# VectorE waits twice for POOL's low parts in the down product, and evicts the first turn ahead of the sums of h

## The reference

```python
def swiglu(h, w_gate, w_up, w_down):
    return (jax.nn.silu(h @ w_gate) * (h @ w_up)) @ w_down
...
    for l in range(DEPTH):
        x = x + 0.5 * swiglu(rms_norm(x, norm_ffn1[l]), ffn1_w_gate[l], ffn1_w_up[l], ffn1_w_down[l])
        ...  # recurrent branch, chunked attention, merge
        x = x + 0.5 * swiglu(rms_norm(x, norm_ffn2[l]), ffn2_w_gate[l], ffn2_w_up[l], ffn2_w_down[l])
```

## Time and profile before

| what | value |
|---|---|
| time, median of 3 runs | 2613.52 us (2612.52 to 2614.4) |
| the profiled execution, its time | 2616.7 us |
| its span, first to last instruction | 2614.9 us |
| granted TensorE clock, mean | 0.994 of full speed |
| PE busy | 2583.0 us, 99% of the span |
| DVE, ACT, POOL busy | 1402.8, 1145.6, 1147.1 us |

### The profile page before, as it was taken

The page is one execution under the profiler, slowest core; times in us unless marked ns, Lnnn a source line. Parts: engine busy times, 40 slices in busy tenths (PEclk is TensorE's granted clock), DMA queues, the critical chain, the costliest instruction groups (busy, mean ns, idle before and its releaser), DMA issues.

```text
span 2614.9 us, 32912 instructions
## 1 busy us (share of the span) xinstructions
PE 2583.0 (99%) x13244; PEld 2168.7 (83%) x13244; DVE 1402.8 (54%) x1949; ACT 1145.6 (44%) x1691; POOL 1147.1 (44%) x458
## 2 busy tenths in 40 slices
PE   9999999999999999999999999999999999999999
PEld 7999787878876788997888988877888778898977
DVE  8767326751346357764187681458413453677720
ACT  5334336743546443334243342467435463433431
POOL 4435544455431344536444354444454314434463
PEclk9999999999999999999999999999999999999999
DMA  5322734433323232422334323253233232424222
GB/s 164 122 73 85 229 91 117 107 96 105 99 73 94 86 113 89 126 69 89 98 91 128 94 69 107 81 134 102 84 110 94 70 100 89 121 68 126 73 93 77
DMA packets 258669, 263.77 MB, mean 101 GB/s; under 512 B 9574, under 2 KB 243174, under 8 KB 258518
## 3 DMA queue, kind: packets, MB, share of 16 engines
q1 hardware_dynamic: 253178, 251.65, 32.1%
q10 hardware_dynamic: 5340, 10.02, 1.3%
HBM read 252.25 MB, written 10.57 MB: 101 GB/s over the span
## 4 chain that ended last, share of the span: by engine, by line
PE 85%; DVE 9%; ACT 2%; POOL 2%; DMA 1%; issue 1%; SPq 0%; ACTq 0%; DVEq 0%
PE ps L1650 21%; PE ps L1654 21%; PE ps L1655 21%; PE ps L1758 4%; PE ps L1763 4%; PE ps L1762 4%; POOL wlo L579 2%; PE ps L1930 1%; PE ps L1988 1%; PE ps L2003 1%; DVE scan L1454 1%; DVE gates L1226 1%; PE ps L1948 1%; PE ps L1952 1%; PE ps L1953 1%; DVE scan L1446 1%
## 5 line engine op out<-in xcount | busy, mean ns | idle before, releaser
L579 POOL TENSOR_TENSOR wlo<-raw,whi 128x1024 fp32r<-128x1024 f32 x386 | 998.0, 2596 | 1029.1 <-ACT whi L623 1029.1
L1650 PE MATMUL ps<-h_lo,whi 128*128 128x512 f32 x1632 | 639.7, 392 | 8.2 <-DVE y L1386 5.6
L1654 PE MATMUL ps<-h_hi,whi 128*128 128x512 f32 x1632 | 637.2, 390 | 0.0
L1655 PE MATMUL ps<-h_hi,wlo 128*128 128x512 f32 x1632 | 637.2, 390 | 0.0
L623 ACT ACTIVATE whi<-raw 128x1024 fp32r<-128x1024 f32 x386 | 403.8, 1053 | 515.7 <-PE ps L1650 456.9
L1650 PEld LDWEIGHTS ps<-h_lo,whi 128*128 128x128 f32 x1632 | 307.5, 188 | 78.1 <-issue 14.2
L1655 PEld LDWEIGHTS ps<-h_hi,wlo 128*128 128x128 f32 x1632 | 307.5, 188 | 64.8
L1654 PEld LDWEIGHTS ps<-h_hi,whi 128*128 128x128 f32 x1632 | 307.6, 189 | 62.6
L1650 PE MATMUL ps<-act_lo,whi 128*128 128x512 f32 x704 | 278.4, 396 | 13.9 <-POOL wlo L579 13.9
L1654 PE MATMUL ps<-act_hi,whi 128*128 128x512 f32 x704 | 277.4, 394 | 0.0
L1655 PE MATMUL ps<-act_hi,wlo 128*128 128x512 f32 x704 | 276.8, 393 | 0.0
(11 more groups left out here) (232 smaller groups left out, 4374.1 us busy)
## 6 DMA issues: line engine op xcount, KB each, us to landing
raw<-in_w_in SPq DMA_DIRECT2D x124, 512.0 KB
raw<-in_w_up SPq DMA_DIRECT2D x88, 512.0 KB
raw<-in_w_down SPq DMA_DIRECT2D x80, 512.0 KB
w_a<-in_w_gate SPq DMA_DIRECT2D x60, 512.0 KB, 5.3
tmp<-in_w_gate SPq DMA_DIRECT2D x20, 512.0 KB, 7.2
rel_band<-rel_rows ACTq DMA_DIRECT2D x1, 8192.0 KB, 39.2
raw<-in_w_up_b SPq DMA_DIRECT2D x16, 512.0 KB
raw<-in_w_out SPq DMA_DIRECT2D x16, 512.0 KB
```

The costliest lines, as they stand in the source:

```text
L579: nc.gpsimd.tensor_tensor(wlo[:, s, :], src, whi[:, s, :].bitcast(F32), ALU.subtract).then_inc(lo_made, 1)
L1650: ins = pe.matmul(ps[:, b, :], w_hi, x_lo, start=start, stop=False)
L1654: pe.matmul(ps[:, b, :], w_hi, x_hi, start=False, stop=False)
L1655: return pe.matmul(ps[:, b, :], w_lo, x_hi, start=False, stop=stop)
```

## The change

ACT's list: the high part of the fifth down chunk moves up, to behind the high parts of tiles 12 to 15; one chunk fewer is then rounded in the loop over the pairs. VectorE's list: after the low parts of tiles 4 to 11 it waits until POOL has counted the low part of the fourth down chunk (`down_low(l, f, AHEAD)` is that count of `lo_made`), then makes the low parts of tiles 12 to 15, then multiplies the four tiles of the last unit as before, then waits for the low part of the fifth down chunk and makes the low parts of tiles 16 to 21. All this in each of the four blocks. `tees` is cut in two: `gains_made` (the eight tiles hx) and `tees` (the sums T and the low part of T2). In the first block alone the second half, and the low part of T1, come after `up_scaled` of the first turn.

```diff
                 act_high(4)
                 ring()
-                act_high(KF - 12)
+                act_high(4)
+                ring()
+                act_high(KF - 16)
                 if behind:
                     behind()
                 for j in range(KD // 2):
-                    ring(len(G22) - (1 if j == 0 else 0) - (AHEAD if ends and j == KD // 2 - 1 else 0))
+                    ring(len(G22) - (2 if j == 0 else 0) - (AHEAD if ends and j == KD // 2 - 1 else 0))
...
+            def down_low(l, f, n):
+
+                first = 4 + UNITS * (UPS + 3)
+                block = first + (KD // 2) * len(G22)
+                return SLOTS + l * (2 * block + MIX_CHUNKS) + f * (block + MIX_CHUNKS) + first + n + 1
...
-            def tees(gain):
+            def gains_made(gain):
 
                 for t in range(KD):
                     nc.vector.tensor_scalar(hx[:, t, :], x[:, t, :], gain(t), None, ALU.mult
                                             ).then_inc(t_step, C.made(t_step))
                 dve.wait_ge(t_step, C.now(t_step))
+
+            def tees():
+
...
-                t_low(T1, 3)
+                if (l, f) != (0, 0):
+                    t_low(T1, 3)
                 for m in range(2):
                     up_scaled(m, 2 + m)
+                if (l, f) == (0, 0):
+                    tees()
+                    t_low(T1, 3)
                 for m in range(2):
                     up_gated(m, m, C.next(silu_made))
...
                     if last:
                         act_low(4, 12)
+                        dve.wait_ge(lo_made, down_low(l, f, AHEAD))
+                        act_low(12, 16)
                     for m in range(4):
                         up_gated(t + m, m, C.next(silu_made, 4) - 1 if m == 0 else C.now(silu_made))
...
-                act_low(12, KF)
+                dve.wait_ge(lo_made, down_low(l, f, AHEAD + 1))
+                act_low(16, KF)
...
-                tees(lambda t: next_gain[:, t:t + 1])
+                gains_made(lambda t: next_gain[:, t:t + 1])
+                if l:
+                    tees()
...
-                tees(lambda t: col("ffn2", t))
+                gains_made(lambda t: col("ffn2", t))
+                tees()
```

## The result

The changed kernel takes 2592.79 us (median of 4 runs, 2590.13 to 2593.64), the kernel before 2613.96 beside it: a ratio of 0.9918, 95% interval 0.9901 to 0.9935, or 21.2 us. Forecast were 2590.3 us and faster. The profiled execution of the changed kernel took 2593.64, its span 2591.8.

A forecast was written before the change was run, and what follows sets the result against it. TensorE, busy 99% of the span, bounds the kernel; its largest wait is for POOL's low parts. 2616.7 - 23.8 + 0.6 = 2593.5 us profiled, 3.2 above the median, so 2590.3 against 2613.52; range 2585 to 2600.

The forecast's parts named there:

- POOL is shut out while VectorE's stream lasts, and a pause lets it in: Fourth down chunk, each block: POOL's subtraction, released by VectorE's wait, ends at 259.90 instead of 268.33 in the first block.
- POOL's longest subtraction near 2.9: Sign that the forecast holds: POOL's longest subtraction takes near 2.9 us and not 11.7.
- The port rule: Skill page: VectorE with two SBUF inputs and GpSimd share a port pair; whoever starts first fully blocks the other for that instruction.
- the margin of 0.2 us: Down product, first block: ACT's fifth high part ready at 259.70, just before POOL ends the fourth low part at 259.90.
- The second rival: Down product: VectorE gets memory first after the fourth low part, later POOL alternates with tiles 16 to 18; 2614 to 2621; chance 0.06.
- VectorE stays ahead: Down product, tiles 16 to 21: VectorE makes one per 0.60 us, TensorE takes one per 0.68, so TensorE sees no cost.
- The first rival: Down product: POOL's sixth and seventh low parts cut between VectorE's instructions; 0.8 us a block, 2593.5 us; chance 0.09.
- The first block: Wait at 45 us goes, first `lo_sum` wait grows from 0.5 to 3.3, 1.7 of low clock follows: loss of 0.6 us.
- the forecast loss: First block's new order: 63.9 against 63.3, a loss of 0.6 us; bounds a gain of 4.4 and a loss of 5.8.
- low clock follows each wait over 2 us: First block: each such wait shown so far was followed by low clock, so 1.7 us was added behind the `lo_sum` wait.
- 23.8 - 0.6 = 23.2: Down product's four waits and their low clock gone, 23.8 us at the most, less the first block's loss of 0.6.
- the four windows: Fourth down chunk in each block, wait included: 10.80, 12.10, 12.20 and 10.60 us, 45.7 in all, against 5.47 each unhindered.

The follow-up runs named there:

- the first block alone: The kernel before with only the first block's new order, without the two pauses and with ACT's list of before: 2613.82 us, ratio 0.9998.

## Why the prediction was right, step by step

- **POOL is shut out while VectorE's stream lasts, and a pause lets it in.** Right. The low part was forecast to end 2.21 after VectorE's last instruction, and ended 2.29 after. Without the pauses it takes 11.68 again, with a gap of VectorE's own 3.30. So the cause is the unbroken stream and not POOL's load, and a gap that VectorE's own wait makes does as well as the pause of 2.32. The forecast sign "POOL's longest subtraction near 2.9" holds for the down product (3.33) and not for the whole kernel: in the first block one takes 5.39 behind the eight `hx`, before and after.
- **The port rule.** The Trainium skill, "SBUF — State Buffer", section "Who interferes with whom", gives the pair to whoever starts first, for the whole instruction. The runs agree that the loser stands still. By that order POOL would have its turn when the instruction ahead of it ends. In a stream without a gap it had not: its subtraction took 11.68 us, and 3.30 with one gap.
- **The fifth low part, and the margin of 0.2 us.** Forecast were ACT's high part 0.28 ahead of the end of POOL's fourth low part; measured 260.22 against 260.60. The second rival didn't happen; putting the rounding late made its alternation and 2624.66 us, inside the expected 2620 to 2631. The early rounding is a condition of the second pause, and the second pause itself does nothing that the time shows.
- **VectorE stays ahead.** Right: no wait for `act_lo`, the sixth and seventh low part in time. The first rival (0.8 us a block) didn't happen: POOL asked for the sixth chunk inside VectorE's last six low parts, and these took 3.69, as unhindered.
- **The first block.** Right in place and near in size: a wait of 0.4 at the eighth chunk (forecast 0.5), 0.90 us idle for SiLU (0.9), the `lo_sum` at 62.38 (62.2), a wait of 2.6 there (2.8), 1.7 of low clock. The 62.38 is in part luck: this execution runs 0.5 late from `hx` on, and the chain gained 1.4 where 1.0 was forecast. The fourth chunk of the down product starts 0.6 later than before (265.4 against 264.8), the forecast loss, but 0.5 of it was there before the new order acts; the first block alone gives a ratio of 0.9998. That evictions cost nothing beside POOL was read from the row at 45.73, ahead of POOL's next start at 47.21, so it didn't show it; the run after does: 1.28 for two at 34.88, while POOL runs from 34.07 to 39.82. That low clock follows each wait over 2 us is no rule: with the first block put back, it did not follow a wait of 2.6. The chain was put to the test: with two multiplications and the idle time out of it, the wait is gone.
- **The size: 2.5 us too much.** For the two profiled executions the sum holds: the span fell from 2614.9 to 2591.8, 23.1 us, where 23.8 - 0.6 = 23.2 was forecast. The step that doesn't hold is the next one, which takes off 3.2 us more to get from the profiled execution to the median. The changed kernel's profiled execution lies 0.85 above its median (2593.64 against 2592.79), not 3.2. The likely reason is that these 3.2 us were in the four windows. The profiled executions of the kernel without pauses (2614.16) and of the first block alone (2613.78) have the same four waits, and lie near their medians. In both, the four windows sum to 42.6 us at clocks of 1.00, 0.84, 0.72 and 0.84, and not to 45.7: 3.1 less, and by the clocks it is low clock that is missing. So what made the profiled execution slow was counted in the 23.8 and taken off once more. With 42.6 - 4 x 5.47 = 20.7 the sum from the median is 2613.96 - 20.7 + 0.6 = 2593.9, against 2592.79 measured. The other 0.4 of the 2.5 is the kernel before, 2613.96 beside the changed one and 2613.52 in the forecast. What the executions without a profile lost isn't shown.

## What to carry to other kernels

Here a subtraction of POOL that took some five times its usual time stood behind VectorE. Where an instruction of POOL takes several times its usual time, look at what VectorE does from its start to its end. If that is a run of instructions with two SBUF inputs and no gap, break it once, at the point where POOL's input is ready, and see to it that POOL has at that moment only as much in hand as VectorE can afford to wait for. Price a wait of TensorE with the low clock behind it, but from more than one execution, and don't add the difference between a profiled execution and the median without asking where it was lost; and where a chain sets a wait, take instructions out of the chain, since moving them inside it moves the wait.

## What the runs showed of the hardware that was not expected

- A pending subtraction of POOL gets in at a gap of VectorE's, even one made by a wait for VectorE's own last instruction: 3.30 us against 11.68. Where VectorE had waited for POOL and POOL's next ones were ready, the two alternated: six low parts in 10.18 us instead of 3.69.
- Whether low clock follows a wait isn't settled by the wait's length. Two windows, of the kernel before and of the changed one, with the same wait of 1.5 us in the recurrent part of layer 0:

```profile
442.00:452.00 10.00, 8.49 (x37) 5.88 (x37) 8.31 (x8) 5.36 (x10) 3.85 (x2) 1.00 0.61 162
```
```profile
442.00:452.00 10.00, 8.48 (x24) 5.84 (x23) 4.43 (x7) 9.10 (x14) 1.96 (x1) 0.66 0.49 132
```

The first ran at 1.00, the second at 0.66, 10 x 0.34 = 3.4 us of clock; and behind a wait of 3.4 the clock stayed at 1.00 in two kernels (without pauses, and the first block alone). What decides it stays open.
- A stretch of low clock is not yet a loss. From the fourth chunk's window of the first block to that of the second, the two executions above took 926.6 and 926.5 us, with the 3.4 us of clock in one of them. In that one the later wait for `y` was shorter, 1.7 instead of 3.1 at the longest, and the low clock behind it, 11 x 0.16 = 1.8 us before, did not come:

```profile
526.00:537.00 11.00, 7.90 (x29) 6.06 (x28) 10.77 (x12) 5.49 (x9) 3.96 (x3) 0.84 0.34 95
```
```profile
526.00:537.00 11.00, 9.31 (x42) 7.40 (x41) 10.73 (x13) 6.46 (x9) 2.77 (x2) 1.00 0.18 56
```

The first block put back as it was shows the same trade the other way round: 1.7 us less of low clock behind one wait, and 1.7 us more of the next wait.
